# Squares summed on VectorE, retention values ahead of gate products, merge splits reordered, single gate loads

## The reference

```python
def rmsnorm(x, g):
    y = x32 * lax.rsqrt(jnp.mean(x32 * x32, axis=-1, keepdims=True) + NORM_EPS)
    return y.astype(x.dtype) * g
...
u = rmsnorm(h, attn_norm_pre[l]);  proj = u @ w_in[l]
...
h = h + rmsnorm(mix, attn_norm_post[l])
f = (silu(z @ ffn_w_gate[l]) * (z @ ffn_w_up[l])) @ ffn_w_down[l]
h = h + rmsnorm(f, ffn_norm_post[l])
...
lbs = jnp.cumsum(jax.nn.softmax(hg_lower_bounds, axis=0), axis=0)
o_ret = retention_mix(q, k, v)
o_ret = head_rms(o_ret).reshape(B, S, RET_HEADS * RET_DV) * jax.nn.silu(rg)
merged = jax.nn.sigmoid(gate_a) * (o_hg @ w_branch_hg) + jax.nn.sigmoid(gate_b) * (o_ret @ w_branch_ret)
x = x + merged @ w_out[l]
...
w = (gb * gelu(x . u_e));  out = sum_e w * v_e
```

## Time and profile before

| | us |
|---|---|
| median of 3 runs | 3425.33 (3425.12 to 3435.29) |
| the profiled execution | 3432.69 |
| its span | 3430.9 |
| TensorE busy in the span | 3323.2 |
| VectorE busy | 1903.7 |
| ScalarE busy | 1251.6 |
| mean granted clock of TensorE | 0.987 of full |

### The profile page before, as it was taken

One profiled execution on the slowest core, in us unless ns is written; L12 is line 12 of the kernel. 1 busy time (PEld: TensorE's weight loads), 2 busy tenths in 40 slices (PEclk: granted clock), 3 DMA queues, 4 the chain that ended last, 5 costly groups with the idle time before them and its releaser, 6 DMA issues.

```text
span 3430.9 us, 50060 instructions
## 1 busy us (share of the span) xinstructions
PE 3323.2 (97%) x18511; PEld 2707.1 (79%) x18511; DVE 1903.7 (55%) x3709; ACT 1251.6 (36%) x1622; POOL 131.7 (4%) x54
## 2 busy tenths in 40 slices
PE   8999999999799999989999999999999999999998
PEld 6676877878577788878878888888887788888886
DVE  4466446442565533342344999988884444444443
ACT  3333233322455333342333333444553333333332
POOL 0000000000000000000000445000000000000000
PEclk9999999999899999999999999999999999999999
DMA  3110013323222222213332444555556655555542
GB/s 135 58 44 2 4 49 98 98 92 98 74 67 73 80 74 73 73 62 98 94 100 80 146 144 141 158 179 183 184 183 220 209 192 194 196 196 193 192 146 80
DMA packets 146028, 408.31 MB, mean 119 GB/s; under 512 B 11224, under 2 KB 43992, under 8 KB 143584
## 3 DMA queue, kind: packets, MB, share of 16 engines
q1 hardware_dynamic: 73520, 265.85, 25.5%
q10 hardware_dynamic: 72368, 140.68, 11.3%
HBM read 337.28 MB, written 69.21 MB: 118 GB/s over the span
## 4 chain that ended last, share of the span: by engine, by line
PE 85%; DVE 11%; ACT 2%; issue 1%; ACTq 1%; DMA 1%; DVEq 0%; SPq 0%
PE bank L333 24%; PE bank L335 23%; PE bank L334 23%; PE bank L929 2%; PE bank L429 2%; PE bank L927 2%; PE bank L362 1%; PE bank L863 1%; ACT arena L970 1%; DVE arena L1961 1%; DVE arena L1924 1%; DVE arena L1925 1%; DVE arena L1927 1%; DVE arena L1959 1%; DVE arena L1926 1%
## 5 line engine op out<-in xcount | busy, mean ns | idle before, releaser
L333 PE MATMUL bank<-xs,ring_hi 128*128 128x512 f32 x2488 | 998.1, 401 | 38.3 <-DVE xs L1454 11.8
L335 PE MATMUL bank<-xs,ring_lo 128*128 128x512 f32 x2488 | 974.3, 392 | 0.0
L334 PE MATMUL bank<-xs,ring_hi 128*128 128x512 f32 x2488 | 973.7, 391 | 0.0
L970 ACT ACTIVATE ring_hi<-ring 128x1024 fp32r<-128x1024 f32 x503 | 531.6, 1059 | 660.8 <-DMA ring<-weights 427.0
L970 ACT ACTIVATE arena<-bank 128x512 f32<-128x512 f32 (+4 forms) x584 | 392.0, 705 | 1013.5 <-PE bank L335 727.4
L1488 DVE TENSOR_TENSOR ring_lo<-ring,ring_hi 128x1024 fp32r<-128x1024 f32 x246 | 299.9, 1224 | 566.0 <-ACT ring_hi L970 564.9
L333 PEld LDWEIGHTS bank<-xs,ring_hi 128*128 128x128 f32 x2488 | 470.4, 189 | 149.8 <-issue 27.0
L335 PEld LDWEIGHTS bank<-xs,ring_lo 128*128 128x128 f32 x2488 | 469.8, 189 | 101.6
L334 PEld LDWEIGHTS bank<-xs,ring_hi 128*128 128x128 f32 x2488 | 471.0, 189 | 99.9 <-issue 5.5
L1974 DVE TENSOR_TENSOR ring_lo<-ring,ring_hi 128x1024 fp32r<-128x1024 f32 x206 | 252.3, 1225 | 385.7 <-ACT ring_hi L970 385.7
L333 PE MATMUL bank<-gw,ring_hi 128*128 128x512 f32 x1024 | 398.5, 389 | 0.7 <-ACT arena L970 0.7
(11 more groups left out here) (279 smaller groups left out, 3391.2 us busy)
## 6 DMA issues: line engine op xcount, KB each, us to landing
ring<-weights SPq DMA_DIRECT2D x503, 512.0 KB, 3.6
hidden<-arena ACTq DMA_DIRECT2D x128, 256.0 KB, 4.1
gates<-arena ACTq DMA_DIRECT2D x16, 2048.0 KB, 6.7
arena<-hidden ACTq DMA_DIRECT2D x16, 2048.0 KB, 10.4
arena<-gates ACTq DMA_DIRECT2D x16, 2048.0 KB, 17.2
xres<-x_t ACTq DMA_DIRECT2D x4, 512.0 KB, 6.8
out_t<-arena SPq DMA_DIRECT2D x4, 512.0 KB, 3.0
arena<-ret_decay ACTq DMA_DIRECT2D x1, 1024.0 KB, 5.6
```

Of the source, the lines that this page charges most:

```text
L333: pe.matmul(out_, wh, x[0], start=start, stop=False, skip_group_check=True)
L334: pe.matmul(out_, wh, x[1], start=False, stop=False, skip_group_check=True)
L335: return pe.matmul(out_, wl, x[0], start=False, stop=stop, skip_group_check=True)
L970: return act.activation(out_, in_, f, **kw)
```

## The change

1. Norms 0, 1, 3 and 5: ScalarE squares tile 0 into an accumulator (`ACC`), VectorE adds the seven others (`add_square`), and TensorE does one ones matmul (`added_sum`) instead of eight. Norm 0's stands behind the second block instead of the first. Norm 1's seven adds, norm 3's and norm 5's stand among VectorE's weight splits.
2. The `lbt` instructions and their `Exp` move ahead of the down projection.
3. Fox and RWKV: six of the 16 transpose groups (tiles 0 to 2 of TA and TB) move into the loop, at units 19, 20, 23, 24, 27 and 28 on TensorE, all in bank 1, with ScalarE's copies at units 20, 21, 24, 25, 28 and 29 behind its `fox_copy`. TensorE's matmul L520 at units 21, 25 and 29 waits for these copies.
4. Retention: the values of j stand ahead of gate product j (j = 1 to 3), in banks 7 and 5 in turn; the squares are added by VectorE, one ones matmul for a head.
5. Merge: the first two sigmoids and weight splits stand behind the 9th and the 14th split of head outputs.
6. Experts: the four loads of groups 0 and 1 are issued ahead of blocks 4, 5, 7 and 9 (hidden 0, hidden 1, gates 0, gates 1), and the loop over eight blocks on ScalarE is written out.

```diff
@@ tensor
+            def added_sum(i):
+                pe.wait_ge(sq_used, (KD - 1) * (i + 1))
+                pe.matmul(bank[SUMS[i]][:, :], cc("ones"), tile(ACC[i]), start=True, stop=True,
+                          skip_group_check=True).then_inc(sum_ready, 1)
...
-                if n == 0:
+                if n == 1:
                     pe.wait_ge(in_cst, 16)
-                    norm_sums(0, KD)
+                    added_sum(0)
...
+                if u in (19, 20, 23, 24, 27, 28):
+                    i, g0 = (u - 19) % 4, (u - 19) // 4
+                    pe.wait_ge(rw_dve, 2 * g0 + 2)
+                    if 2 * g0 + i:
+                        pe.wait_ge(tok_out, 2 * g0 + i)
+                    for g in range(TT):
+                        tr = pe.transpose(bank[1][:, g * P:(g + 1) * P], tile((TA, TB)[i] + g0)[:, g * P:(g + 1) * P], cc("ident"))
+                    tr.then_inc(tok_ready, 1)
                 if u in (17, 21, 25, 29):
                     pe.wait_ge(rw_dve, 2 * m + 1)
+                    if m:
+                        pe.wait_ge(tok_out, 2 * m)
                     pe.matmul(bank[1][:, :], cc("bones"), tile(RKR), start=True, stop=True).then_inc(rw_pe, 1)
...
                 w_out_block(b)
-                for k in {4: (0, 1), 5: (2, 3), 7: (4, 5, 6, 7)}.get(b, ()):
-                    norm_sum(1, k)
+            added_sum(1)
...
-                if k:
-                    norm_sum(3, k - 1)
-            norm_sum(3, KD - 1)
+            added_sum(3)
             norm_sums(4, KD)
...
+                product(q + 8, [(B_RET + 8, KD)], XS, h, 12, 12)
+                values(0)
+                for j in range(1, 4):
+                    values(j)
+                    product(q + 8 + j, [(B_RET + 8 + j, KD)], XS, h, 12, 12)
+                pe.wait_ge(rt_sum, h * 4 + 4)
+                pe.matmul(bank[4][:, :], cc("ones"), tile(R_["SQ"]), start=True, stop=True).then_inc(rt_pe, 1)
...
@@ scalar
+                if u in (20, 21, 24, 25, 28, 29):
+                    i, g0 = (u - 20) % 4, (u - 20) // 4
+                    act.wait_ge(tok_ready, 2 * g0 + i + 1)
+                    A(tile((MA, MB)[i] + g0), bank[1][:, :], ACT.Copy).then_inc(tok_out, 1)
...
+                gate(0)
+                for j in range(4):
+                    b = bank[(7, 5)[j % 2]]
+                    act.wait_ge(rt_pe, h * 13 + 8 + j + 1)
+                    st.go(A(arena[:, bass.ds(h * 4 + (ORET + j), 1), :].rearrange("p a t -> p (a t)"), b[:, :], ACT.Copy))
+                    if j >= 2:
+                        act.wait_ge(rt_sum, h * 4 + j)
+                    A(tile(R_["SQ"] if j == 0 else SQ2 + j % 2), b[:, :], ACT.Square).then_inc(rt_act, 1)
+                    if j:
+                        gate(j)
...
             for k in range(24):
                 if k == 9:
                     act.wait_ge(rt_dve, 12 * RET_H + 1)
+                    merge_gate(0)
+                if k == 14:
+                    merge_gate(1)
                 A(OHL[k][0], tile(OHG + k), ACT.Copy).then_inc(o_hi_ready, 1)
...
-            load(0)
-            load(1)
-            with act.Fori(1, NU_REST // 4 - 1) as i:
-                for b in range(4):
-                    expert_hi(n + b, i, 4)
-                    gelu(B_U + j0 + b, q + b, j0 + b, i, 4)
+            for b in range(4, NU_REST - 4):
+                if b in (4, 5):
+                    load_part(0, b - 4)
+                if b in (7, 9):
+                    load_part(1, (b - 7) // 2)
+                expert_hi(n + b)
+                gelu(B_U + j0 + b, q + b, j0 + b)
@@ vector
+            def add_square(i, k):
+                ve.wait_ge(sq_ready, KD * i + k + 1)
+                if k > 1:
+                    ve.wait_ge(sq_used, (KD - 1) * i + k - 1)
+                TTN(tile(ACC[i]), tile(ACC[i]), tile(NORM[i][0] + k % 2), ALU.add).then_inc(sq_used, 1)
...
             dense(1)
+            dense(2)
+            for k in range(1, KD):
+                add_square(0, k)
+            dense(3)
...
             for k in range(24):
+                if k in (9, 14):
+                    dense(B_MERGE + (3 if k == 9 else 4))
                 ve.wait_ge(o_hi_ready, k + 1)
```

164 lines of the change are left out of this document (96 added, 68 removed).

## The result

The changed kernel takes 3392.9 us (median of five, 3389.8 to 3412.3) against 3430.9 us of the kernel before on the same chip (median of five, 3425.1 to 3435.3). The ratio is 0.9899, with a 95% interval of 0.9879 to 0.9918: the medians are 38.0 us, or 1.1%, apart. The forecast was 3373.7 us, a gain of 51.6; the measured median lies 1.9 us above the upper end of the range.

A forecast was written before the change was run, and what follows sets the result against it. TensorE, busy 3323.2 of 3430.9 us, was taken as the bound. Eight terms summed to -51.6 us, taking the profiled 3432.7 to 3381.1; less 7.4 to the median gave 3373.7 us, range 3358 to 3391.

The forecast's parts named there:

- the term of the fox loop: Fox loop: 9.4 us more in the loop, 4.0 less behind it, together 5.4 us more.
- rival (d): Fox loop: waits for ScalarE push TensorE to 1.2 GHz, through the RWKV stage; up to 170 us more, 3544; chance 0.04.
- Norm 0: First norm: block 1 starts early, one sum follows VectorE's adds, and block 2 starts near 26.4 us: 7.5 us less.
- Norm 1: Norm at the last w_out product: four sums go (3.4 us), one add of 0.81 joins the chain: 2.6 us less.
- Norm 3 and lower bounds: Around the down products: seven sums go (6.0), the last comes 0.9 later, the reciprocal 2.5 sooner: 7.6 us less.
- Retention and merge: Retention: 3.85 us less per head, 15.4 in all; merge: fewer splits ahead of product D, 7.8 us less.
- Norm 5: Norm 5: six sums saved, the last hidden again among the products, 0.2 us lost: 4.9 us less.
- Gate loads: Expert blocks: loads issued singly no longer block ScalarE, so TensorE's waits and low clock there go: 11.2 us less.
- (a): The fox loop hides the transposes, so its term is -4.0 instead of +5.4 us: 3364.3; chance 0.14.
- (b): Gate loads only spread the jam; perhaps 3 of 11.2 us are gained: 3381.9; chance 0.13.
- (c): Adds and hand-overs come later than thought at norms 1, 3, 5 and in retention: some 10 us, 3384; chance 0.10.
- (e): Whole change: in each place something else was late by as much; within 0.3%, near 3425; chance 0.03.

The follow-up runs named there:

- fox_alone: The kernel before with only the fox part of the change, six of sixteen by-token transposes and their copies inside the loop: 3450.7 us, ratio 1.0055.
- fox_as_before: The changed kernel with its fox loop and the sixteen transpose groups behind it as in the kernel before: 3370.5 us, ratio 0.9818.
- after_again: The changed kernel run once more, unaltered: 3396.9 us.
- copies_unit_earlier: The changed kernel with ScalarE's by-token copies made one unit of the loop earlier: 3372.8 us, in a second run 3373.4 us.
- loads_alone: The kernel before with the change's gate and hidden loads alone: 3419.9 us, ratio 0.9967.

## Why the prediction was off, point by point

**The step that failed is the term of the fox loop.** I had it at +5.4 us. It is +16.7 (`fox_alone` against before) to +22.4 (changed kernel against `fox_as_before`) by the medians, and +19.0 (`after_again`) to +21.7 (`fox_alone`) in the traces behind unit 17. That makes 35 to 40 us of the 57.0 us of gain, where 38.0 were measured. The mechanism stood in the prediction as rival (d), with a chance of 0.04 and at a price of up to 170 us: it was right that the waits for ScalarE push TensorE to 1.2 GHz, and wrong in two ways on the size. It does not reach into the RWKV stage: in the two traces of the changed kernel the clock is back at 1.00 at 332 and 313 us, ahead of the first RWKV product at 337.60 and 323.98, and stays there to 400 us, although TensorE waits in that stage as well. And it is not all or nothing: behind the waits the low level holds for 34 (`after_again`) to 44 us (`fox_alone`) in all, in parts of 7 to 21 us. The mistake was to give the two outcomes "5.4 us" and "170 us" and nothing between them. Where each matmul takes up to twice as long, 34 to 44 us at the low level cost up to half of themselves, 17 to 22 us, which is what was measured; a range meant to hold the rivals had to hold some of that.

The ground that I gave against (d) was poor: the 1.27 us wait in retention that left the next matmul at 1.12 us. That wait stands once in 85 us, between products that keep TensorE full. In the fox loop a wait of 1.30 us was followed by the low level within 2.5 us. A single row from another stage doesn't say what the clock does here. And the row of the matmul right behind a wait says nothing of (d) in any stage: in `fox_alone` the transposes and scores right behind the wait ran at full speed too (0.63 and 1.12), and the fall came 2 us later. It takes the granted clock of the next stretch; in the kernel before that is 1.00 from 1238 to 1248 us, so that the wait in retention did leave the clock up, but only this shows it. The traces did have a row that spoke for (d), which I had not read: the kernel before shows 0.57 at 230 to 240 us in this very loop.

The waits themselves I had placed and sized well: at the second transposes and at the bones matmul, at units 20/21, 24/25 and 28/29. I had L540 at 264.3 in place of 260.7, 3.6 us later; in `after_again`, counted from unit 17, it is 4.3 later (17.6 against 13.3), with waits of 0.95 and 1.62 at the high level. What was mis-sized is what follows a wait, which the term put at nothing.

**Norm 0.** -7.5 forecast; the sum ends at 25.25 + 1.10 = 26.35, my 26.4, and everything up to the fox loop comes 7.8 us sooner: right.

**Norm 1.** -2.6 forecast; -3.7 and -4.4 from the loop's end to the feed-forward net. This stretch holds the RWKV stage too, so that I can't split it finer. TensorE does wait 3.22 us for the last add, of which I had seen only 0.81 as a new link. I had also counted only the four sums ahead of the last product; seven are gone, 7 x 0.86 - 3.22 = 2.8, so that two errors of the term cancel.

**Norm 3 and lower bounds.** -7.6 forecast; -7.3 and -7.6. The last sum waits 3.08 us where it waited 1.43, 1.65 more against my 0.9, and ran at the low level in some traces (2.07 us). The part of the lower bounds shows by itself: the wait ahead of the first HGRN product fell from 9.05 to 6.50 us, 2.55 against my 2.5.

**Retention and merge.** -15.4 and -7.8, together -23.2; both traces show -24.1. The head's period fell by 4.1 (3.85 forecast), and the second branch product starts 8.0 us behind the first split (7 forecast; the first one ran in part at the low level). That root and splits come later in retention did no harm: no wait of TensorE stands there. The drain behind a table load that the Trainium skill (ScalarE: Activation LUTs, What ACT_TABLE_LOAD costs) would add could not be seen: with or without it, the slack held.

**Norm 5.** -4.9 forecast, -5.2 in both: seven sums less (6.0) and a wait of 0.86 us, where I had counted six sums and 0.2.

**Gate loads.** -11.2 forecast; -11.4 in both traces, and -11.1 alone. The reason, ScalarE's blocked issue, is shown by the issue rows (397 and 606 ns at most, 9717 before). ScalarE's wait for a store, 4.8 us in the earlier trace rows, went as well. The Trainium skill (DMA: Bandwidth & Descriptors, Queues, rings and completion order) has descriptors taken in ring order, but lets a later one finish its write sooner; it is the semaphore's increment that comes after the earlier writes. What that seemed to threaten here, stores held up by loads, cost nothing that these rows show.

**The base.** I counted from 3425.3, the median of three; over all the chip runs here the kernel before has medians of 3430 to 3436. Of the 19.2 us between forecast and measurement 5.6 are this base, and 13.6 are gain that is missing. Against its own round's 3434.0 the gain without the fox part, 63.5 us (3434.0 - 3370.5), was somewhat more than the 57.0 forecast.

**The other rivals.** (a), the loop hides the transposes, is what `copies_unit_earlier` does in its traces (-4.0 and -3.5 from unit 17 on), but not with the copies where the change put them. (b), the loads only spread the jam, and (c), late adds and hand-overs, are out: each of their terms was met within 1.8 us in the traces, (b) also by `loads_alone`. (e) is out by the measurement, and by `fox_as_before`. And the part of the clock that is not the change's, how long it stays low from unit 13 on, was in no rival: the loop's end lies 7 and 14 us apart in the two pairs of traces of one kernel.

**Chances.** "Faster by over 0.3%" was given 0.93 and came. The signs promised for the sums, block 2, the head's period, product D and the issues all came; "the transposes behind the fox loop start near 304 instead of 295" failed: they start at 329.6.

## What to carry to other kernels

Before putting work into a loop in which TensorE is nearly full, ask of each new semaphore who of the other engine's program stands ahead of its increment: a copy that ScalarE makes behind the same unit's work makes TensorE wait about 1 us, and the same copy one unit earlier in the program cost nothing in two traces. Price such a wait by what the granted clock does behind it, not by its own length; 4 to 7 us of waits cost 17 to 29 here. A cheap guard is a table of PEclk by stretches of 10 us before and after, ahead of any reading of single rows, and a test that takes the waits alone.
